# Eight gate products of a two-half transformer block, taken from behind attention into its steps

## The reference

```python
x = x + 0.5 * swiglu(rms_norm(x), w_gate, w_up, w_down)          # 1024 -> 2816 -> 1024
h = rms_norm(x)
q_lat, kv_lat, k_rope, fq, fk, fv, f_logit, g_mla, g_fox = split(h @ w_in)
y_mla = mla_mixer(q_lat, kv_lat, k_rope, ...)    # 8 heads, 96 wide keys, causal softmax
y_fox = fox_mixer(fq, fk, fv, f_logit, ...)      # 8 heads, 64 wide, with a forget decay
mixed = sigmoid(g_mla + b0) * (y_mla @ w_branch_mla) + sigmoid(g_fox + b1) * (y_fox @ w_branch_fox)
x = x + mixed @ w_o
x = x + 0.5 * swiglu(rms_norm(x), w_gate2, w_up2, w_down2)
```

## Time and profile before

| | us |
|---|---|
| median of 3 runs | 2533.37 (2526.28 to 2536.85) |
| profiled execution, its own time | 2537.6 |
| span of that execution | 2535.8 |
| TensorE / VectorE busy | 2139.5 / 1812.1 |
| ScalarE / GpSimd busy | 1178.1 / 745.8 |

### The profile page before, as it was taken

How to read it: one execution, slowest core, us unless ns; L and a number is a source line. 1 busy time by engine, 2 the same in 40 slices (tenths; PEclk the granted TensorE clock), 3 DMA queues, 4 the chain that set the end, 5 groups by cost and what they waited for, 6 DMA issues and landing times.

```text
span 2535.8 us, 28491 instructions
## 1 busy us (share of the span) xinstructions
PE 2139.5 (84%) x9496; PEld 1516.8 (60%) x9496; DVE 1812.1 (71%) x3312; ACT 1178.1 (46%) x3774; POOL 745.8 (29%) x634
## 2 busy tenths in 40 slices
PE   6987898988777778998755697999739989998999
PEld 6965443433222227873434484786339977797997
DVE  6975767778888887888898968675665546546454
ACT  5224555656666664432455543333244435344442
POOL 0002344454554543233555533332310002000000
PEclk9988999999999998999866598999969989799999
DMA  5112999999999998999998999999945542124453
GB/s 208 67 67 97 392 390 413 412 421 421 421 421 420 416 408 343 399 420 395 370 364 319 369 420 421 376 421 421 378 188 188 185 148 88 67 99 167 160 189 133
DMA packets 107458, 760.86 MB, mean 300 GB/s; under 512 B 12064, under 2 KB 12832, under 8 KB 16432
## 3 DMA queue, kind: packets, MB, share of 16 engines
q0 software_dynamic: 73728, 536.90, 52.1%
q1 hardware_dynamic: 33584, 222.15, 23.1%
HBM read 756.91 MB, written 2.10 MB: 299 GB/s over the span
## 4 chain that ended last, share of the span: by engine, by line
PE 42%; DVE 9%; DMA 5%; issue 3%; ACT 2%; POOL 1%; DVEq 0%; ACTq 0%
PE bank L551 41%; DMA pair<-in_uv,idx 5%; DVE resid L963 4%; DVE pair L1519 2%; DVE half L957 1%; DVE tmp L957 1%; PE bank L923 0%; PE bank L571 0%; ACT frow L1593 0%; ACT half L1593 0%; DVE smalls L1236 0%; POOL pair L2104 0%; DVE smalls L1309 0%; POOL smalls L2059 0%; DVE ft_lo L957 0%
## 5 line engine op out<-in xcount | busy, mean ns | idle before, releaser
L2104 POOL DMA_INDIRECT pair<-in_uv,idx x512 | 641.7, 1253 | 901.5 <-DVE resid L963 573.1
L1593 ACT ACTIVATE smalls<-smalls 128x1 f32<-128x1 f32 x2058 | 540.2, 286 | 669.3 <-DVE smalls L1519 651.0
L1519 DVE CUSTOM_DVE_ANT_0 pair<-pair,hn 128x1024 f32<-128x1024 f32 x512 | 623.5, 1219 | 174.8 <-DMA pair<-in_uv,idx 173.1
L551 PE MATMUL bank<-pair,diag 128*128 128x512 f32 x928 | 459.3, 627 | 120.2 <-ACT diag L1593 119.4
L551 PEld LDWEIGHTS bank<-pair,diag 128*128 128x128 f32 x928 | 168.5, 194 | 392.7 <-ACT diag L1593 247.1
L551 PE MATMUL bank<-ft,raw 128*128 128x256 f32 x1664 | 365.7, 383 | 11.9 <-DVE ft L957 11.9
L963 DVE SCALAR_TENSOR_TENSOR resid<-pair,smalls,resid 128x1024 f32<-128x1024 f32 x280 | 358.1, 1279 | 0.6 <-ACT smalls L1593 0.3
L551 PEld LDWEIGHTS bank<-ft,raw 128*128 128x128 f32 x1664 | 320.3, 193 | 57.2 <-issue 12.7
L957 DVE TENSOR_TENSOR half<-raw,half 128x1024 fp32r<-128x1024 f32 (+1 forms) x204 | 235.0, 1193 | 136.3 <-ACT half L1593 136.3
L551 PE MATMUL bank<-ft_hi,half 128*128 128x256 f32 x1664 | 299.0, 282 | 6.4 <-DVE ft_lo L957 6.4
L1593 ACT ACTIVATE half<-raw 128x1024 fp32r<-128x1024 f32 (+1 forms) x204 | 199.7, 1029 | 153.9 <-PE bank L551 145.9
(11 more groups left out here) (256 smaller groups left out, 2709.3 us busy)
## 6 DMA issues: line engine op xcount, KB each, us to landing
raw<-in_wts SPq DMA_DIRECT2D x196, 1024.0 KB, 6.1
pair<-in_uv,idx POOLq DMA_INDIRECT x512, 11.2
raw<-in_wts SPq DMA_DIRECT2D x10, 512.0 KB, 6.2
raw<-in_wts SPq DMA_DIRECT2D x4, 720.0 KB, 6.2
resid<-in_x SPq DMA_DIRECT2D x4, 512.0 KB, 6.7
out<-resid SPq DMA_DIRECT2D x8, 256.0 KB, 5.7
raw<-in_wts SPq DMA_DIRECT2D x2, 768.0 KB, 7.1
rowt<-in_rows SPq DMA_DIRECT2D x1, 1076.0 KB, 12.4
```

The source lines that it names most:

```text
L551: return e.matmul(o, a, b, start=start, stop=stop)
L1519: e.tensor_tensor_reduce(b[:, 0:1024], b[:, 0:1024], HN[i // 128], 1.0, 0.0, ALU.mult, ALU.add, actv[:, i % 8:i % 8 + 1]).then_inc(dotted, 1)
L1593: return e.activation(o, i, f, **kw)
L2104: e.indirect_dma_start(pair[i % NPAIR], None, uv, bass.IndirectOffsetOnAxis(ap=idx[:, n % SLOTS, k:k + 1], axis=0)).then_inc(pairs_in[i % ...
```

## The change

- The gates' products go into `attention`. Gate chunk 0 stands in front of the first look. Chunks 1 to 7 are cut in two halves of 128 channels each, placed at the steps of a table `GATE_AT`, behind the transposition of that step; three of the fourteen halves stand behind the last look.
- The gate sums are taken out of PSUM with their bias but without the sigmoid (`gate_in`), and three wide sigmoids come in one pass after attention. `sig` becomes three tiles per half of the block (`sigA`, `sigB`), placed where memory is free during attention.
- The splits of B's gate chunks and of two branch chunks stand at the steps of `SPLIT_AT` in attention; before, only one split stood there.
- mla's products `q`, `k` and their transpositions move from steps 0, 2, 5, 8 and 6, 9, 12, 14 to 0, 3, 6, 9 and 11, 14, 18, 21, on all engines, and the bank order `PREP` goes with them.
- The branches run fox first, then mla, and wait for transpositions `fin` two by two.
- In B VectorE takes out and scales fox's transposed keys; before, ScalarE did.
- Gate chunk 0 is loaded before mla's two weight chunks. `PACE` and the planned times change: 86 steps instead of 84 between the start of attention's stage and FFN 2.

```diff
-            + [(("fqkv", i, p), 2048) for i in range(6)] + [(("qb", 0, p), 1536), (("kvb", 0, p), 1024)]
-            + [(("gate", i, p), 2048) for i in range(8)] + [(("br", i, p), 2048) for i in range(4)]
+            + [(("fqkv", i, p), 2048) for i in range(6)] + [(("gate", 0, p), 2048)]
+            + [(("qb", 0, p), 1536), (("kvb", 0, p), 1024)] + [(("gate", i, p), 2048) for i in range(1, 8)] + [(("br", i, p), 2048) for i in range(4)]
...
-PACE = ((64, 3.85), (25, 3.3), (54, 2.2), (30, 3.75), (64, 3.85), (PAIRS, 2.6))
+PACE = ((64, 3.85), (25, 3.3), (28, 2.1), (36, 2.85), (22, 2.6), (64, 3.85), (PAIRS, 2.6))
...
-PREP = {("q", 0): 0, ("k", 0): 2, ("tq", 0): 4, ("q", 1): 6, ("tk", 0): 8, ("k", 1): 10, ("tq", 1): 12, ("tk", 1): 14}
+PREP = {("q", 0): 0, ("k", 0): 2, ("tq", 0): 4, ("tk", 0): 6, ("q", 1): 8, ("k", 1): 10, ("tq", 1): 12, ("tk", 1): 14}
+
+GATE_AT = {"A": {1: (16, 17), 2: (23, 24), 3: (25, 26), 4: (27, 28), 5: (29, 30), 6: (31, 32), 7: (33, 34)},
+           "B": {1: (7, 8), 2: (16, 17), 3: (23, 24), 4: (25, 26), 5: (27, 28), 6: (30, 32), 7: (34, 36)}}
+
+SPLIT_AT = {2: ("fqkv", 5), 14: ("gate", 0), 17: ("gate", 1), 20: ("gate", 2), 25: ("gate", 3), 27: ("gate", 4),
+            29: ("gate", 5), 33: ("gate", 6), 37: ("gate", 7)}
...
-        p.add("look" + x, [0, 1] * 16, 3.2)
+        p.add("gate" + x, [4] if x == "A" else [5, 5], 6.0)
+        p.add("look" + x, [0, 1] * 8, 3.3)
+        p.add("look" + x, [0, 1] * 8, 6.2)
         p.add("turn" + x, [2, 3] * 16)
         p.add("prep" + x, [6, 7] * 8)
         for blk in range(4):
             p.add("o" + x, [4 + blk % 2], told=False)
-            p.add("fin" + x, [4 + blk % 2], 4.0)
+            p.add("fin" + x, [4 + blk % 2], 2.0)
+            if blk in (1, 2):
+                p.add("gate" + x, [3 + blk])
+        p.add("gate" + x, [6, 7, 6, 7, 6] if x == "A" else [6, 7, 6, 7])
         p.at = 0
-        for stage, n, us in (("gate", 8, 7.0), ("br", 16, 1.8), ("wo", 4, 7.0)):
+        for stage, n, us in (("br", 16, 1.8), ("wo", 4, 7.0)):
...
+                attention(p, ft)
                 for c in range(4):
-                    yt = yf if c % 2 else ym
-                    if c == 0:
-                        for blk in range(4):
+                    yt = ym if c % 2 else yf
+                    if c < 2:
+                        for blk in (2 * c, 2 * c + 1):
                             taken(e, "fin" + p, blk)
...
-                if n in (0, 6):
-                    i = n // 6
+                if n in (0, 11):
...
-                if n in (5, 12):
-                    e.wait_ge(qm_done, 4 * nth + 2 * (n // 12) + 1)
-                    heads_turned(stage, PREP["tq", n // 12], 96, QM[0])
-                if n in (8, 14):
-                    e.wait_ge(qm_done, 4 * nth + 2 * (n // 14) + 2)
...
+                if n in (6, 18):
+                    e.wait_ge(qm_done, 4 * nth + 2 * (n // 18) + 1)
+                    heads_turned(stage, PREP["tq", n // 18], 96, QM[0])
+                if n in (9, 21):
+                    e.wait_ge(qm_done, 4 * nth + 2 * (n // 21) + 2)
+                    heads_turned(stage, PREP["tk", n // 21], 96, QM[1])
...
+                def gate(c, j):
+
+                    w = piece(("gate", c, p), 8)
+                    o, done = fresh("gate" + p, c) if j == 0 else (bank[B["gate" + p, c].bank], full[B["gate" + p, c].bank])
+                    for kt in range(8):
+                        ins = by(o[:, j * HALF:(j + 1) * HALF], w(kt, slice(j * P, (j + 1) * P)),
+                                 ft(kt, slice(0, HALF)), kt == 0, kt == 7)
+                    if j:
+                        ins.then_inc(done, 1)
+
+                for j in range(2):
+                    gate(0, j)
...
+                    for c, at in GATE_AT[p].items():
+                        if n in at:
+                            gate(c, at.index(n))
...
-                    if n == 10:
-                        split(after(("fqkv", 5, p)))
+                    if n in SPLIT_AT:
+                        split(after((*SPLIT_AT[n], p)))
...
+                for j in range(4 if p == "B" else 0):
+                    i, q = divmod(j, 2)
+                    o, out_ = filled(e, "tfk" + p, j)
+                    ts(KFT[p][0:66, 4 * q:4 * q + 4, i * P:(i + 1) * P], four(o[0:66, :]), col("fk", 0, 66), None,
+                       ALU.mult).then_inc(out_, 1)
...
+                        sg = SIG[p][8 - 8 * (c % 2) + n]
+                        e.wait_ge(sig_done, 3 * nth + 3)
                         tt(sg, sg, o[:, 0:HALF], ALU.mult).then_inc(out_, 1)
...
+            def gate_in(p, c):
+
+                o, out_ = filled(e, "gate" + p, c)
+                act(SIG[p][2 * c], o[:, 0:HALF], ACT.Identity, bias=col("bg", 2 * c)).then_inc(s_step, ss.up())
+                act(SIG[p][2 * c + 1], o[:, HALF:2 * HALF], ACT.Identity, bias=col("bg", 2 * c + 1)).then_inc(out_, 1)
...
-                    if n == 10:
-                        rounded(after(("fqkv", 5, p)))
+                    if n == 2:
+                        gate_in(p, 0)
+                    for c, at in GATE_AT[p].items():
+                        if n == at[1] + 1:
+                            gate_in(p, c)
+                    if n in SPLIT_AT:
+                        rounded(after((*SPLIT_AT[n], p)))
...
-                for i in range(2):
+                for i in range(2 if p == "A" else 0):
...
+                yield when("fin" + p, 3)
+                e.wait_ge(s_step, ss.n)
                 for c in range(8):
-                    yield when("gate" + p, c)
-                    o, out_ = filled(e, "gate" + p, c)
-                    act(SIG[:, 2 * c, :], o[:, 0:HALF], ACT.Sigmoid, bias=col("bg", 2 * c)).then_inc(s_step, ss.up())
-                    act(SIG[:, 2 * c + 1, :], o[:, HALF:2 * HALF], ACT.Sigmoid, bias=col("bg", 2 * c + 1)).then_inc(out_, 1)
-                    rounded(after(("gate", c, p)))
+                    taken(e, "gate" + p, c)
+                for piece in SIGS[p]:
+                    act(piece, piece, ACT.Sigmoid).then_inc(sig_done, 1)
```

More of the change, by code:

```diff
@@ L434, in program @@
         YMT = ar("ymt", LAYER + 2048, 1024).rearrange("p (k t) -> p k t", k=4)
-        SIG = ar("sig", LAYER + 4096, 4096).rearrange("p (g t) -> p g t", g=16)
+        SIGS = {x: [ar(f"sig{x}{i}", LAYER + a, 256 * n) for i, (a, n) in enumerate(places)]
+                for x, places in (("A", ((12544, 2), (3072, 4), (6144, 10))), ("B", ((9728, 4), (3072, 2), (6144, 10))))}
+        SIG = {x: [s[:, a:a + 256] for s in pieces for a in range(0, s.shape[1], 256)] for x, pieces in SIGS.items()}
         MT = ar("mt", LAYER, 2048).rearrange("p (k t) -> p k t", k=8)
@@ L839, in chain @@
                     e.transpose(o[:, 2 * P:3 * P], LAT[:, i, 192:320], idt[:]).then_inc(done, 1)
-                attention(p)
-                for c in range(8):
-                    w = piece(("gate", c, p), 8)
-                    o, done = fresh("gate" + p, c)
-                    for j in range(2):
-                        for kt in range(8):
-                            ins = by(o[:, j * HALF:(j + 1) * HALF], w(kt, slice(j * P, (j + 1) * P)),
-                                     ft(kt, slice(0, HALF)), kt == 0, kt == 7)
-                    ins.then_inc(done, 1)
+                attention(p, ft)
                 for c in range(4):
-                    yt = yf if c % 2 else ym
-                    if c == 0:
-                        for blk in range(4):
+                    yt = ym if c % 2 else yf
+                    if c < 2:
+                        for blk in (2 * c, 2 * c + 1):
                             taken(e, "fin" + p, blk)
@@ L883, in prepared, with attention @@
                         mm(o[:], KLT[:, sl], w(0, slice(h * 512, (h + 1) * 512)), True, True).then_inc(done, 1)
[L884 to L892 removed]
+                if n in (6, 18):
[4 more added lines that the diff above has]
+                    heads_turned(stage, PREP["tk", n // 21], 96, QM[1])
+            def attention(p, ft):
+                t0, nth = T0[p], NTH[p]
+                def gate(c, j):
[8 more added lines that the diff above has]
+                    gate(0, j)
                 for i in range(2):
@@ L1399, in chain @@
                 split(after(("fqkv", 4, p)))
+                for j in range(4 if p == "B" else 0):
[3 more added lines that the diff above has]
+                       ALU.mult).then_inc(out_, 1)
                 yield from attention(p)
-                for c in range(8):
-                    split(after(("gate", c, p)))
                 for c in range(4):
@@ L1781, in prepared @@
                 stage = "prep" + p
-                if n in (1, 7):
-                    i = n // 7
+                if n in (1, 12):
+                    i = n // 12
                     for h in range(2):
@@ L1922, in chain @@
                         e.wait_ge(mt_sum, n + 1)
-                        act(MT2[0][:, n, :], SIG[:, n, :], ACT.Copy).then_inc(mt_hi, 1)
```

(3 more changed lines are left out.)

44 lines of the change are left out of this document (21 added, 23 removed).

## The result

| | before | changed |
|---|---|---|
| median (lowest to highest), 7 runs each | 2531.94 (2526.28 to 2537.13) | 2517.23 (2512.21 to 2518.81) |
| ratio, 95% interval | | 0.9939 [0.9923, 0.9954] |
| span of the profiled execution | 2535.8 | 2517.0 |
| start of A's first FFN to the start of the tail | 911.1 | 905.9 |
| of it from A's second FFN on | 282.0 | 273.0 |

A forecast was written before the change was run, and what follows sets the result against it. The woven stretch was taken as DMA-bound after the change, the tail as TensorE work, waits and low clock. Gains of 15.5 + 5 (woven) and 11 (tail), 32 us, gave 2505.6, as median 2501; own range 2490 to 2513.

The forecast's parts named there:

- I take 271.5 + 10 = 281.5: Woven stretch, A's attention to second FFN: DMA floor 271.5 us plus 10, against 297 before, a gain of 15.5 us.
- The first 16 looks: First part of A's attention: 28 rows, 70 us on VectorE, 90 with chain work and waiting, while DMA needs 80.
- The remaining looks, drain, branches and w_o have gates beside them and are DMA's: Rest of the woven stretch, behind the first 16 looks: bound by DMA, no loss added.
- The 4.5 us wait: A's attention: the 4.5 us wait for the last attention output remains in either kernel if its cover goes.
- Rival (b): Woven stretch gives nothing, as looks behind gate halves or late weights stop VectorE's rows; only the tail's 11: 2522, chance 0.14.
- Behind the start of the second FFN: Gathered rows left behind A's second FFN: two fewer, a gain of 5 us.
- mla's wider distances: A's attention: mla's rows wider apart remove part of VectorE's 9.2 us of waits for TensorE; inside the 10, not added.
- The tail: Half B alone: upper gain 26.4 us, less 6 for splits, 8 for low clock, 1.5 for the drain, so 11.
- Rival (a): TensorE's clock stays up with gates inside attention: tail gains 19, A 30, together 49 us, 2484; chance 0.15.
- Rival (d): Gates themselves run at 1.2 GHz: tail loses 19 us, A 34 against 21 won, together +32, 2565; chance 0.06.
- Rival (c): Tail gives nothing, as nine splits at 2.4 us each eat 22 of 26; only A's 21 us: 2512, chance 0.12.
- under 380 GB/s: Sign that the forecast is wrong: A's stretch still moves under 380 GB/s.

The follow-up runs named there:

- late: Changed kernel, but at step 11 of half A mla's second query product stands behind the product with the values: median 2510.9 us, ratio to before 0.9913.
- drain: Changed kernel, but half A's six attention steps behind the last look fall due 3.3 us apart on VectorE and ScalarE: 2509.84 us, ratio to before 0.9902.
- prep_old_a: Changed kernel, but in half A mla's products and transpositions are back at their old steps: 2515.78 us, ratio to before 0.9925.
- the second profile: The changed kernel, unaltered, profiled again beside the first three experiments: median 2515.8 us, ratio to before 0.9934.
- b_only: Kernel before with the change in half B (the tail) only, branches fox first in both halves: 2515.94 us, ratio to before 0.9937.
- scale_late: Changed kernel with the edits of drain and late, and VectorE's scalings of mla's queries and keys in half A one step later: 2501.97 us, ratio to before 0.9878.
- pow_apart: scale_late plus the sigmoid pass starting with fox's gates, and GpSimd's two powers of mla's queries made in two steps, both halves: 2504.77 us, ratio to before 0.9870.

## Why the prediction was wrong, point by point

- **The failed step is "I take 271.5 + 10 = 281.5".** The amount and the floor were right (272); the 10 was 28. It was the sum of two parts, and both were too small.
  - "The first 16 looks": 90 us where DMA needs 80, so 10 (32 MB at 420 GB/s are 76, not 80). They took 87 us, to step 16 at 1383.6, but at 354 GB/s; these 30.7 MB need 73, so 13.6. A wait of 5.7 us for TensorE stands in them; `late` shows 2 to 4 us as its price. The kernel before had given a warning: 314 GB/s in 1320 to 1400 was 20 of the 30.5 us that it stayed above its floor, in steps that only one of chunks 1 to 7 reaches. I had read only 20 us of it and the mean of 161 us, and counted 20.5 of the 30.5 as what gates fill.
  - "The remaining looks, drain, branches and w_o have gates beside them and are DMA's" was put at nothing and came to 14.5: 5.3 in 1383.6 to 1400 at 284 GB/s, 6.9 in 1500 to 1520, 2.3 in the rest. It took the full DMA of the stage behind attention as a property of the place. With the gates gone from it VectorE's queue had nothing between, and stood 12.3 us for the last outputs and 5.2 for the sigmoids. The 4.5 us wait did not "remain": it grew to 12.3, and `drain` shows 6 to 8 us as its price.
- **Rival (b)** named the mechanism, a gate half that stops VectorE's row work through TensorE, and was wrong about the place: the outputs, not the looks. No late weight was seen. It said 2522; the changed kernel at 2517.2 lies about a quarter of the way from there to the forecast 2501.
- **Behind the start of the second FFN**: 5 us forecast, 9.0 measured. 103.78 MB instead of 106.94 were left, so three rows and not two: the stage issued 91 gathers instead of 89, and one more (360 for 359) stood ahead of it. This hid part of the fault.
- **mla's wider distances**: inside the 10, near nothing; prep_old_a agrees.
- **The tail**, 11 forecast, 12.8 measured (13.2 in the second profile, b_only 15.6), and its terms fit within 1.3 us each: splits 6, waits for turned probabilities and splits 4.3 + 1.1 = 5.4; low clock 8, 14.66 busy us at 0.54 cost 14.66 x 0.46 = 6.7; drain 1.5, TensorE idle 0.4 of 22 us behind attention. The three fall short of the forecast by 3.0 us. Rival (a), a clock that stays up, did not come: in the changed tail TensorE was busy 14.66 of 15 us and still at 0.54. The Trainium skill, "TensorE: Matmul & The Clock Gate" (HAM oscillation), has gaps bring the half rate back and work without gaps keep the full rate. The spell began behind TensorE's wait of 3.70 us and the 81 us at 1.00 followed without one over 1.2, which agrees; that the clock stayed low through 15 us with 14.66 busy does not.
- **Rival (d)**, gates at 1.2 GHz: hardly so. In the tail the clock was 1.00 from 2163 on, and one half gate began in the spell ahead of that. In A ten of the fourteen halves took 3.62 us, their time at full clock, and four took 5.1 to 5.9 behind waits: 7.3 us more in all, against the 47 that (d) counted. Rival (c) falls with the tail's gain. Of my own signs, "under 380 GB/s" in A's stretch was met only in its first part (369; 381 over all), and the other two, splits over 10 us and spells over 35, did not come.

## What to carry to other kernels

Price a filling of idle DMA time window by window: length times (1 - rate / full rate), and count only the windows in which the moved work will stand; the rest of the deficit has another cause. And ask what filled the windows that are full today, for the moved work may have been it. When work is put ahead of a product on one engine, look at who waits for that product on an in-order queue that carries other work too, and when it is sent there: here due times spread by 3.3 us were worth half as much as the whole change. A stop removed by reordering the producer can come back on a third engine, so look at all waits of the shared queue, not at the one that was removed.

## What the runs showed of the hardware

- TensorE's clock fell behind a wait and stayed low while TensorE was nearly gapless again. In the changed tail a wait of 3.70 us was followed by 14.66 busy us of 15 at 0.54, then 14.00 of 14 at 1.00. In A a wait of 5.60 us was followed by 0.50 from 1490 to 1496. In the kernel before, the spells of the tail began behind waits of 1.68 us (2153.4) and 2.43 us (2187.0).
- The gathers' rate follows GpSimd's queue within a few us, although seven row buffers exist. After 4.6 us without an issue (scale_late, powers) it was 0 and 8 GB/s in two slices of 1 us; after a pause of 3.2 us for a buffer (pow_apart) it was 82 and 0. That most of the buffers were waiting for VectorE at such a time is inferred from GpSimd's waits for VectorE just before (4.45 and 0.67 us in scale_late), not seen.
